# Two attention stages and two delta-rule stages in one block, each hand-over with a wait of its own

## The reference, cut to what matters

```python
h = x * (1 + scale) + shift
proj = h @ w_in
# mixer A: softmax attention, 3 groups (window, dilation) = (128,1), (512,4), (2048,16), 4 heads of 64
s = einsum(q, k) * dh**-0.5 - slopes * steps * dilation      # masked
p, lse = softmax_with_lse(s);  o = einsum(p, v)              # groups are combined later by their denominators
# mixer B: gated DeltaNet, 6 heads, d_k = d_v = 128
sol = triangular_solve(eye(C) + lower, rhs);  u, w = sol[..., :dv], sol[..., dv:]
v_new = u - w @ S
o = (q * exp(G)) @ S + intra @ v_new
S = S * exp(g_last) + (k * exp(g_last - G)).T @ v_new
# merge
merged = sigmoid(gA) * branch_a + sigmoid(gB) * branch_b
x_new = layer_norm(alpha * x + gate * (merged @ w_o))
```

## Time and profile before

| | |
|---|---|
| median of three runs | 2465.42 us |
| span of the profiled execution | 2465.2 us |
| PE busy | 2349.4 us (95%) |
| DVE busy | 1587.2 us (64%) |
| ACT busy | 1130.7 us (46%) |
| POOL busy | 268.0 us (11%) |
| mean granted TensorE clock | 0.974 of full |
| stretch 1576 to 1635 (`attend_samples`) | PE 45.6 busy of 59 us, DMA share 0.82 |
| stretch 1635 to 1912 (`delta_prompt`) | PE 254.6, DVE 222.4 busy of 277 us |

### The profile page before, as it was taken

The page is one execution under the profiler, slowest core; times in us unless marked ns, Lnnn a source line. Parts: engine busy times, 40 slices in busy tenths (PEclk is TensorE's granted clock), DMA queues, the critical chain, the costliest instruction groups (busy, mean ns, idle before and its releaser), DMA issues. The chain is left out here.

```text
span 2465.2 us, 45107 instructions
## 1 busy us (share of the span) xinstructions
PE 2349.4 (95%) x16926; PEld 2076.6 (84%) x16926; DVE 1587.2 (64%) x4065; ACT 1130.7 (46%) x2381; POOL 268.0 (11%) x461
## 2 busy tenths in 40 slices
PE   5999999999999999999999899889999799999998
PEld 2777788888999999999999867558888699999886
DVE  6867676454454767767544377668986777665665
ACT  4544444443422544444444376637776533332333
POOL 0000000000111111110000000233321111111000
PEclk8999999999999999999999999989999799999999
DMA  7222323333422332233333281975665655556443
GB/s 261 95 112 94 112 103 103 117 120 104 164 98 80 107 108 92 91 108 101 116 106 106 92 324 47 346 227 144 165 172 181 211 171 177 174 161 218 136 147 99
DMA packets 231305, 350.78 MB, mean 142 GB/s; under 512 B 47782, under 2 KB 167182, under 8 KB 225840
## 3 DMA queue, kind: packets, MB, share of 16 engines
q1 hardware_dynamic: 174672, 217.09, 28.3%
q0 software_dynamic: 34400, 119.40, 12.6%
q10 hardware_dynamic: 22016, 11.40, 1.6%
HBM read 240.45 MB, written 107.39 MB: 141 GB/s over the span
## 5 line engine op out<-in xcount | busy, mean ns | idle before, releaser
L305 PE MATMUL ps_f<-m_lo,w_hi 128*128 128x272 f32 (+1 forms) x2436 | 790.1, 324 | 12.8 <-DVE m_lo L615 6.2
L305 PE MATMUL ps_f<-m_hi,w_hi 128*128 128x272 f32 (+1 forms) x2436 | 793.7, 326 | 0.0
L305 PE MATMUL ps_f<-m_hi,w_lo 128*128 128x272 f32 (+1 forms) x2436 | 785.4, 322 | 0.0
L305 PEld LDWEIGHTS ps_f<-m_lo,w_hi 128*128 128x128 f32 x2436 | 459.1, 188 | 67.6 <-issue 32.1
L305 PEld LDWEIGHTS ps_f<-m_hi,w_lo 128*128 128x128 f32 x2436 | 459.8, 189 | 36.9
L305 PEld LDWEIGHTS ps_f<-m_hi,w_hi 128*128 128x128 f32 x2436 | 459.1, 188 | 33.8
L679 DVE TENSOR_TENSOR stage<-partial,ps_f 128x512 f32<-128x512 f32 (+2 forms) x348 | 171.5, 507 | 318.5 <-PE ps_f L305 307.0
L430 ACT ACTIVATE partial<-ps_f 128x272 f32<-128x272 f32 (+1 forms) x348 | 160.8, 462 | 392.7 <-PE ps_f L305 390.9
L392 ACT ACTIVATE w_hi<-w_raw 128x512 fp32r<-128x512 f32 x348 | 213.1, 625 | 204.4 <-PE ps_f L305 128.1
L586 DVE TENSOR_TENSOR w_lo<-w_raw,w_hi 128x512 fp32r<-128x512 f32 x348 | 239.1, 688 | 85.2 <-ACT w_hi L392 81.7
L704 DVE SCALAR_TENSOR_TENSOR conv<-stage,side,conv 128x1024 f32<-128x1024 f32 x108 | 138.4, 1281 | 8.1 <-ACT conv L446 6.8
(11 more groups left out here) (531 smaller groups left out, 4449.0 us busy)
## 6 DMA issues: line engine op xcount, KB each, us to landing
w_raw<-in_w_feat SPq DMA_DIRECT2D x58, 1024.0 KB, 5.8
gates<-scratch_g_d SPq DMA_DIRECT2D x56, 256.0 KB, 3.2
z_f<-scratch_z_d ACTq DMA_DIRECT2D x13, 768.0 KB, 4.7
scratch_conv_d<-conv POOLq DMA_DIRECT2D x18, 544.0 KB, 3.0
scratch_conv_d<-conv POOLq DMA_DIRECT2D x18, 512.0 KB, 2.9
kc<-in_k_cache SPq DMA_DIRECT2D x8, 1152.0 KB, 15.8
vc<-in_v_cache POOLq DMA_DIRECT2D x8, 1152.0 KB, 13.2
w_ada<-in_w_ada SPq DMA_DIRECT2D x8, 1024.0 KB, 14.9
```

The costliest lines, as they stand in the source:

```text
L305: last = pe.matmul(out[:, 0:n], l[:, cols], r, start=start and k == 0 and nth == 0, stop=k == KH - 1 and nth == 2, skip_group_check=not start)
```

## The change

The four stages are given one block, `attend_and_delta`. The functions take that block as an argument and open none of their own, so each engine branches from the end of one stage's part to the begin of the next without meeting the others. No computing instruction and no DMA is added, removed or moved within its engine. The three places where a barrier kept stages apart get these waits:

- attend_prompt to attend_samples: POOL waits for the `q_bd` products (its own, which PE waited for already) before it clears `coef`, for the prompt's last scores before the values of samples 2 to 4, and for the prompt's last weighing before the values of samples 5 to 7.
- attend_samples to delta_prompt: PE waits for the masks of chunks 0 and 1 before the Gram matrices of chunk 2, and for the samples' last outputs (`samples_put`) before those of chunk 3. DVE waits for the last transposes of half 1 before its solve goes on, POOL for the samples' last weighing before it clears `TT`.
- delta_prompt to delta_samples: POOL waits for the last use of G, the last solution and the last coupling, PE for `bv`, ACT for the stored gate.

```diff
@@ -1029,7 +1029,7 @@
 
-def attend_prompt(nc, t, first, late, pair, g_last):
+def attend_prompt(nc, t, block, first, late, pair, g_last):
 
@@ -1066,8 +1066,7 @@
         stats_stored = sem("stats_stored")
-        late.update(rows_out=row_stored, stats_out=stats_stored)
-        block = ctx.enter_context(nc.Block(name="attend_prompt"))
+        late.update(rows_out=row_stored, stats_out=stats_stored, prompt_scored=s_full[1], prompt_weighed=o_full)
 
@@ -1357,7 +1356,7 @@
 
-def attend_samples(nc, t, late, ab, coef, eps_o, pair):
+def attend_samples(nc, t, block, late, ab, coef, eps_o, pair):
 
@@ -1397,6 +1396,7 @@
         row_put, row_out = sem("g_row_put"), sem("g_row_out")
+        pair.update(samples_turned=t_full, samples_attended=attended, samples_put=att_put)
         W = NHB * NBLK
@@ -1407,7 +1407,6 @@
         over = lambda s: s.unsqueeze(1).broadcast_to([P, NB, NHB])
-        block = ctx.enter_context(nc.Block(name="attend_samples"))
 
@@ -1440,10 +1439,12 @@
         def _(pool):
+            pool.wait_ge(q_put, 1 + 4 * NG)
             pool.memset(coef[:, :, :, :], 0.0).then_inc(cleared, 1)
...
                     pool.dma_start(vc[:, s], t["v_cache"][s]).then_inc(v_in[s // HALF], 16)
+            pool.wait_ge(late["prompt_scored"], NG * NBLK)
             values(2, 3, 4)
@@ -1454,6 +1455,7 @@
             pool.dma_start(t["G_rows"].rearrange("b (h p) -> (b h) p", p=P), G_row[:, :]).then_inc(row_out, 16)
+            pool.wait_ge(late["prompt_weighed"], NG * NBLK)
             values(5, 6, 7)
@@ -2079,7 +2081,7 @@
 
-def delta_prompt(nc, t, coef, late, pair, sc, tail, e):
+def delta_prompt(nc, t, block, coef, late, pair, sc, tail, e):
 
@@ -2107,12 +2109,12 @@
 
+        gate_in, gate_full, gate_put, gate_out = late["gate_in"], sem("gate_full"), sem("gate_put"), sem("gate_out")
         zeroed = sem("d_zeroed")
...
         o_out, o_last, s_out = [sem(f"o_out{j}") for j in range(2)], sem("o_last"), sem("s_out")
-        late.update(o_out=o_out, o_last=o_last, s_out=s_out)
         G_loaded, sub_ready = pair["G_loaded"], [pair["sub_ready"], sem("sub_ready1")]
@@ -2123,8 +2125,7 @@
         qs_put, vn_put = sem("qs_put"), sem("vn_put")
-        gate_in, gate_full, gate_put, gate_out = late["gate_in"], sem("gate_full"), sem("gate_put"), sem("gate_out")
-        block = ctx.enter_context(nc.Block(name="delta_prompt"))
+        late.update(o_out=o_out, o_last=o_last, s_out=s_out, gate_out=gate_out, G_used=G_used, sub_out=sub_out, YT64=YT64)
 
@@ -2266,6 +2267,7 @@
                 pool.tensor_tensor(ET[c % 2][:, :, :], G_in[c % 2][:, :, :], heads2(causal_T), ALU.add).then_inc(G_used, 1)
+            pool.wait_ge(pair["samples_attended"], 2)
             pool.memset(TT[0][:, :, :, :], 0.0).then_inc(zeroed, 1)
@@ -2459,7 +2461,10 @@
                 if it == -1:
-                    grams(a), grams(a + 1)
+                    pe.wait_ge(masked, 6)
+                    grams(a)
+                    pe.wait_ge(pair["samples_put"], 8)
+                    grams(a + 1)
                     turn_keys(b)
@@ -2579,6 +2584,7 @@
                 if it == -1:
+                    dve.wait_ge(pair["samples_turned"], 2 * (-(-KT_C // 4) + 1))
                     for piece in range(BEFORE, 8):
@@ -2768,7 +2774,7 @@
 
-def delta_samples(nc, t, coef, late, eps_o, tail, s_kept, e):
+def delta_samples(nc, t, block, coef, late, eps_o, tail, s_kept, e):
 
@@ -2793,7 +2799,6 @@
         of_bank = lambda b, k: bank[t_bank[b][k]].rearrange("p (a n) -> p a n", n=P)
-        block = ctx.enter_context(nc.Block(name="delta_samples"))
         c = {n: coef[0:R, NBLK, k, :] for k, n in enumerate(COEF)}
@@ -2824,6 +2829,9 @@
         def _(pool):
+            pool.wait_ge(late["G_used"], NBLK)
+            pool.wait_ge(late["sub_out"], 16 * (NBLK // 2))
+            pool.wait_ge(late["YT64"], NBLK)
             pool.dma_start(tail["ident"][:, :], t["ident"]).then_inc(tail_in, 16)
@@ -2850,6 +2858,7 @@
             ac.wait(pe, "k_T")
+            dv.wait(pe, "bv")
             pe_.done(per_head(1, R, lambda out, h: mm(out, k_T[:, h, :], k_T[:, h, :])), "gk")
@@ -2944,6 +2953,7 @@
             act.wait_ge(late["o_last"], 16)
+            act.wait_ge(late["gate_out"], 64)
             for j in range(2):
@@ -3789,22 +3799,23 @@
-        with ExitStack() as inner:
...
-                attend_prompt(nc, t, head, late, pair, g_last)
-                attend_samples(nc, t, late, ab, coef, eps_o, pair)
...
-                delta_prompt(nc, t, coef, late, pair, sc, tail, e)
-                delta_samples(nc, t, coef, late, eps_o, tail, s_kept, e)
+        with nc.Block(name="attend_and_delta") as block:
+            with ExitStack() as inner:
...
+                    attend_prompt(nc, t, block, head, late, pair, g_last)
+                    attend_samples(nc, t, block, late, ab, coef, eps_o, pair)
...
+                    delta_prompt(nc, t, block, coef, late, pair, sc, tail, e)
+                    delta_samples(nc, t, block, coef, late, eps_o, tail, s_kept, e)
         renew()
```

More of the change, by code:

```diff
@@ L3791, in program @@
         tail["third_in"] = nc.alloc_semaphore(name="third_in")
[L3792 to L3807 removed]
+        with nc.Block(name="attend_and_delta") as block:
+            with ExitStack() as inner:
+                coef = inner.enter_context(nc.sbuf_tensor("coef", [P, NBLK + 1, len(COEF), NHB], F32))
+                pair = first_pair(nc, t, inner)
+                with ExitStack() as early:
+                    top = (nc.sbuf_usable_end - nc.sbuf_base) // 32 * 8 - P
+                    early.enter_context(nc.sbuf_tensor("below_ident", [P, top], F32))
+                    pair["ident"] = early.enter_context(nc.sbuf_tensor("ident_top", [P, P], F32))
+                with ExitStack() as both:
+                    late = sample_inputs(nc, t, both, pair, head)
+                    attend_prompt(nc, t, block, head, late, pair, g_last)
+                    attend_samples(nc, t, block, late, ab, coef, eps_o, pair)
+                with ExitStack() as both:
+                    late = state_inputs(nc, t, both)
+                    e = sample_places(nc, t)
+                    delta_prompt(nc, t, block, coef, late, pair, sc, tail, e)
+                    delta_samples(nc, t, block, coef, late, eps_o, tail, s_kept, e)
         renew()
```

11 lines of the change are left out of this document (removed).

## The result

The changed kernel took 2472.67 us (median of 14 runs, 2466.41 to 2483.26) against 2465.27 us of the kernel before beside it (14 runs, 2461.12 to 2471.8): ratio 1.0025, 95% interval 1.0014 to 1.0036, so 3.5 to 8.9 us slower. Forecast were +0.9 us and a range up to 2470.4. The profiled execution has a span of 2471.3 us, the one before 2465.2, both at a mean granted clock of 0.974. PE was busy for 2350.1 us against 2349.4, so of the 6.1 us between the two spans 5.4 are idle time of PE. Of these 6.1 us, 2.9 lie ahead of everything that the change touches (next paragraph).

The account below looks back on a forecast made before the run. It took PE, busy 95% of the span, to bound the kernel, with DMA full from 1578 on. Terms +1.6 - 0.3 - 0.4 = +0.9 us on 2465.4 gave 2466.3 us, range 2460.6 to 2470.4.

Parts of the forecast that it names:

- Early starts of PE and POOL, and the three barriers: At the three stage borders: barrier idles vanish; PE's scores start 4.5 us earlier, POOL's first values at 1578.0 instead of 1582.3.
- Seam 1, "taken +1.6": attend_prompt to attend_samples: stream and clock make the solve start +0.2 to +2.4 us later, taken as +1.6.
- Both transfers end together ... at 1591.9: att_T stores and values of samples 2 to 4 share the DMA engines, both ending after 12.2 us, at 1591.9.
- my two bounds: att_T stores beside values: packet for packet, stores end at 1591.9 (chosen); equal bytes, stores end at 1587.
- keys land 1605.1, and the Gram matrices start at 1605.2, as now: Chunks 0 and 1: the stream is 2.4 us later, keys land at 1605.1, Gram matrices start unchanged at 1605.2.
- "I take 1.4" for the clock: Gram matrices of chunks 0 and 1: PE's idle ahead lowers the granted clock, costing 1.4 us (0 to 5.4).
- the slower rival: Before the Gram matrices: stream hole as forecast, clock low through all 24 matmuls, +5.4 instead of 1.4; 2470.3 us, chance 0.17.
- From the masks to the solve: POOL's system stores follow the masks, behind values of samples 5 to 7 up to 2.4 us later; counted within +1.6.
- From the solve on: After the solve's start: the delay is carried along; everything behind the delta_prompt to delta_samples border is PE's, unchanged.
- Seams 2 and 3, -0.7: attend_samples to delta_prompt gives -0.3 us, most hidden by the solve; delta_prompt to delta_samples gives -0.4 us.

Follow-up runs that it names:

- e1: Changed kernel with POOL's loads of the values of samples 2, 3 and 4 moved behind its waits for the stores of att_T; ratio 1.0013 to the kernel before.
- e3: Changed kernel with the barrier between the two attention stages kept, attend_samples and both delta-rule stages in one block; ratio 0.9994 to the kernel before.
- e11: Changed kernel with only sample 2's values loaded ahead of POOL's waits for the att_T stores, samples 3 and 4 behind; ratio 1.0023 to the kernel before.
- e12: Changed kernel with the last four att_T stores cut by partitions (8 KB rows) instead of by tokens (2 KB rows); ratio 1.0018 to the kernel before.
- e2: Changed kernel with only the two attention stages in one block, barriers kept ahead of delta_prompt and delta_samples; ratio 1.0024 to the kernel before.
- e4: Changed kernel with SP's last store of the statistics put behind its last att_T stores instead of ahead; ratio 1.0027 to the kernel before.
- e5: Changed kernel with POOL loading keys and queries of chunks 0 and 1 before its wait for the stores and all values; ratio 1.0000 to the kernel before.
- e14: Kernel before, barriers kept, with the values of samples 5 to 7 issued only when sub_u has landed; ratio 1.0049 to the kernel before.
- e9: e5 with ACT instead of POOL storing the second half of the masked systems and SP loading all of sub_u; ratio 0.9997 to the kernel before.

## Why the prediction was wrong, step by step

- **Early starts of PE and POOL, and the three barriers**: right, to 0.1 us (scores at q+0.1, first values at q+1.1, no idle at seams 2 and 3).
- **Seam 1, "taken +1.6"** at the start of the solve, is the term that failed, by its size: measured +6.2. Of these, 2.6 are the later start of the Gram matrices (forecast 0), 1.7 the clock (forecast 1.4), 1.9 the way from the masks to the solve (forecast 0.2). The next four points take them one by one.
- **"Both transfers end together ... at 1591.9"** is the step in it that went wrong. It put POOL's next load at 1593.8, q+16.8; measured q+20.5. The parts: the values' data began at q+2.1, where I had q+2.7 (-0.6); I let 0.6 MB of the stores pass alone ahead of the values, and none did, because the statistics' packets were still ahead of them (0.6 MB at 352 GB/s, +1.7); I moved the rest at 413 GB/s on average, and between 1582 and 1598 it was 352 (5.6 MB in 16 us; 5.04 MB in 14.3 instead of 12.2, +2.1), as 185 in the first 2 us, 274 in the last 2 and 392 between; from 1598 to POOL's issue it took 2.3 us instead of 1.9 (+0.4). Packet for packet, the choice between my two bounds, was right. That both end together was not: the values were through by 1594, and the stores ended with the lump.
- **"keys land 1605.1, and the Gram matrices start at 1605.2, as now"**: followed from it, and failed with it: q+30.8 instead of q+28.2, +2.6.
- **"I take 1.4" for the clock**: +1.73 in the changed kernel, +1.5 in e1. Right. What I held against the slower rival, that only the seam before had no matmuls right ahead of its idle, was not: PE worked up to 1601.2 here and the granted clock still stands at 0.50 from 1604, and at the seam before PE had matmuls up to 1575.85 as well.
- **From the masks to the solve**, counted within the +1.6: the masks ended 4.3 us late (q+38.9), the solve 6.2. The 1.9 between are the stores of the systems, behind and beside the values of samples 5 to 7, now later: 24 KB each, they took a median of 6.8 us to land from POOL and 8.0 from SP, where it was 5.0 and 5.5. I had named POOL's queue and given it no term of its own, and SP's stores beside it none at all.
- **From the solve on**, the delay was to be carried along. Up to the state it was: +6.2 at the solve, +6.5 at the first state matmul, because in this kernel the solve was the later branch (PE idle 5.94 us behind DVE's masks at L2322). That weigh(1) is a second branch, which decides as soon as the solve is early, was not seen. Behind it the pair of profiles does not bear it out: +1.5 at L2991 (q+336.9 against q+335.4) and +3.2 at the end. The spans differ by 6.1 only because q came 2.9 us later. From the first state matmul to the last chunk's, before and then after, PE was 5.4 us less busy at a higher clock (0.96 against 0.93):

```profile
1652.33:1901.78 249.45, 233.10 (x2671) 213.18 (x2669) 204.37 (x1080) 173.52 (x570) 66.72 (x92) 0.93 0.63 176
```

```profile
1661.66:1906.53 244.87, 227.70 (x2670) 207.99 (x2668) 203.69 (x1080) 173.74 (x570) 66.13 (x92) 0.96 0.64 178
```

Whether that is the change or the clock's own scatter, one profile each can't tell. That the 6.2 us at the solve and the 6.2 us by the ratio agree is in part luck.
- **Seams 2 and 3, -0.7**: e3 has -1.5 us with an interval from -4.4 to +1.5; consistent, not shown.
- The slower rival (hole, and the low clock through all 24 matmuls, 2470.3) had the right sign and came nearest, but not by its mechanism: the low clock cost 1.7 and not 5.4, the hole and the stores behind it 4.5 and not 0.2.

What stays open: why e1 and e11, with POOL on 7 to 11 us earlier, gain so little of the time; what the statistics ahead of `att_T` cost by themselves; and how much of the loss comes by the clock elsewhere. The runs' spans go with their mean clock (1.5 us for each 0.001), and the changed kernel's mean clock was lower by 0.0027, give or take 0.0014; at equal clock 3.0 us of its 7.0 us (difference of the mean spans) are left. So more than half of the loss goes with a lower mean clock. The two profiles, both at 0.974, do not show where it was lower, and whether the change lowers it was not tested.

## What to carry to other kernels

A barrier can be holding back transfers as well as engines. Before it is taken away, go through each queue and ask what is now issued earlier than a transfer that something waits for: the lump of both must land before the waiter goes on. Then let the engine that starts earlier find its next input first in the queue (here the keys: 1.0025 became 1.0000), and look for the place where two branches meet before pricing a gain on one of them.

## What the runs showed of the hardware

- Two DMA queues took turns packet by packet whatever their packets' size: 161 to 162 with 9 KB against 2 KB, 113 to 106 with 9 KB against 8 KB.
- Where SP's stores had not begun when the values' data came, they began only after some 7 to 8 packets of the software queue on each engine (131 in the changed kernel, 125 in e12, 115 in e11), some 4 us, although SP had issued its first store before POOL its first load. In e2 and e4, whose stores had begun before the values, it did not happen.
- Small stores beside 9 KB loads were slow on both kinds of queue: stores of 24 KB took a median of 12.0 us to land from POOL's software queue, where the loads stood ahead of them, and also 12.0 us from SP's hardware queue, where none did (e5); with no values under way it was 2.0 and 1.5 us (e14). All on hardware queues, beside the same loads, they kept SP from loading `sub_u` until q+39.6, 12 us after the masks (e9).
